# Streaming encoder on one core: order of the value products, of the first chunk's transfers and of the tail's convolution taps

## What is computed

```python
u = rmsnorm(x, g) @ w_in                     # 11 groups of 256 columns
a_b, a_c, a_x, a_g, b_v, b_a, b_g, c_u, c_g, x_q, x_g = split(u, 11)
y_a = a_b * conv3(a_c * a_x) * silu(a_g)
y_b = silu(layernorm(conv31(b_v * sigmoid(b_a)) + bias)) * silu(b_g)
y_c = (pool_linear(trailing_means(c_u) - c_u) + bias) * scale * silu(c_g)
y_x = softmax(q @ K.T / 8) @ V * silu(x_g)   # 4 heads, 256 memory tokens
y   = rmsnorm(x + concat(y_a, y_b, y_c, y_x) @ w_out, g_final)
```

## Time and profile before

| | |
|---|---|
| median of 3 runs | 1570.24 us (1567.27 to 1572.03) |
| the profiled execution | 1572.66 us |
| its span, first to last instruction | 1570.8 us |
| TensorE busy | 1447.3 us, 92% |
| VectorE busy | 1221.1 us, 78% |
| ScalarE, GpSimd busy | 566.9 us (36%), 234.0 us (15%) |
| TensorE's mean granted clock | 0.975 of full |

### The profile page before, as it was taken

One profiled execution on the slowest core, in us unless ns is written; L12 is line 12 of the kernel. 1 busy time (PEld: TensorE's weight loads), 2 busy tenths in 40 slices (PEclk: granted clock), 3 DMA queues, 4 the chain that ended last, 5 costly groups with the idle time before them and its releaser, 6 DMA issues.

```text
span 1570.8 us, 32694 instructions
## 1 busy us (share of the span) xinstructions
PE 1447.3 (92%) x11758; PEld 1238.1 (79%) x11758; DVE 1221.1 (78%) x3102; ACT 566.9 (36%) x1250; POOL 234.0 (15%) x188
## 2 busy tenths in 40 slices
PE   5877699999999999999999999999999999999995
PEld 4755587878787887878787887878787887878784
DVE  7996396886969696886969597886869697796856
ACT  7763232333324332342323332332333332333333
POOL 2251011111101111111001111111001111111110
PEclk9988799999999999999999999999999999999998
DMA  9875355555354556545354556445354556446373
GB/s 271 227 282 191 122 175 197 187 178 196 107 223 139 182 188 202 183 155 224 105 217 145 174 187 214 174 155 231 106 195 159 181 187 214 170 140 229 98 251 128
DMA packets 129827, 286.26 MB, mean 182 GB/s; under 512 B 12554, under 2 KB 70590, under 8 KB 129790
## 3 DMA queue, kind: packets, MB, share of 16 engines
q1 hardware_dynamic: 129789, 285.77, 53.6%
HBM read 226.65 MB, written 59.08 MB: 182 GB/s over the span
## 4 chain that ended last, share of the span: by engine, by line
PE 45%; DVE 26%; issue 14%; DMA 8%; ACT 2%; SPq 1%; POOL 1%; DVEq 1%; ACTq 0%; POOLq 0%
DVE z L1363 9%; PE u L524 7%; PE u L525 7%; PE u L526 7%; DMA pt<-probs_turned 4%; PE qps L524 4%; PE qps L526 4%; PE qps L525 4%; PE sps L524 4%; PE sps L526 4%; PE sps L525 4%; DVE prow L1387 3%; DMA probs_turned<-probs 3%; DVE xb L1291 2%; DVE probs L292 1%
## 5 line engine op out<-in xcount | busy, mean ns | idle before, releaser
L524 PE MATMUL u<-h_hi,w_hl 128*128 128x256 f16 (+1 forms) x2992 | 795.7, 272 | 12.1 <-ACT gate L872 7.3
L525 PE MATMUL u<-h_lo,w_hl 128*128 128x256 f16 (+1 forms) x2992 | 794.4, 271 | 0.0
L526 PE MATMUL u<-h_hi,w_hl 128*128 128x256 f16 (+1 forms) x2992 | 793.9, 271 | 0.0
L1363 DVE SCALAR_TENSOR_TENSOR z<-glu,cst,z 128x256 f32<-128x256 f32 (+1 forms) x1020 | 425.1, 488 | 0.5
L524 PEld LDWEIGHTS u<-h_hi,w_hl 128*128 128x128 f16 x2992 | 295.4, 99 | 63.7 <-issue 12.6
L526 PEld LDWEIGHTS u<-h_hi,w_hl 128*128 128x128 f16 x2992 | 295.6, 99 | 34.7
L525 PEld LDWEIGHTS u<-h_lo,w_hl 128*128 128x128 f16 x2992 | 295.6, 99 | 33.3
L872 ACT ACTIVATE gate<-u,inv 128x256 f32<-128x256 f32 (+1 forms) x204 | 83.0, 458 | 169.6 <-PE u L526 169.0
L524 PE MATMUL sps<-ring,y_hi 128*128 128x512 f32 (+1 forms) x278 | 112.4, 404 | 16.8 <-POOL y_lo L1805 14.3
L526 PE MATMUL sps<-ring,y_lo 128*128 128x512 f32 (+1 forms) x278 | 110.2, 396 | 0.0
L525 PE MATMUL sps<-ring,y_hi 128*128 128x512 f32 (+1 forms) x278 | 109.8, 395 | 0.0
(11 more groups left out here) (222 smaller groups left out, 1911.6 us busy)
## 6 DMA issues: line engine op xcount, KB each, us to landing
ring<-wo_split SPq DMA_DIRECT2D x256, 512.0 KB, 6.8
ob<-in_x_prompt SPq DMA_DIRECT2D x34, 512.0 KB, 4.3
probs_turned<-probs SPq DMA_DIRECT2D x130, 128.0 KB, 2.4
pt<-probs_turned SPq DMA_DIRECT2D x32, 512.0 KB, 3.4
out<-ob SPq DMA_DIRECT2D x32, 512.0 KB, 3.5
rows_turned<-rows SPq DMA_DIRECT2D x122, 128.0 KB, 2.4
w_hl<-in_w_in SPq DMA_DIRECT2D x20, 512.0 KB, 7.3
wo_split<-ring SPq DMA_DIRECT2D x16, 512.0 KB, 5.1
```

The source lines that it names most:

```text
L524: nc.tensor.matmul(out, a_hi, b_hi, start=first, stop=False)
L525: nc.tensor.matmul(out, a_hi, b_lo, start=False, stop=False)
L526: return nc.tensor.matmul(out, a_lo, b_hi, start=False, stop=last)
L1363: ins = nc.vector.scalar_tensor_tensor(z[:, c, 0:n], glu[:, c, k:k + n], w, z[:, c, 0:n], ALU.mult, ALU.add)
```

## The change

It moves steps and waits; nothing is computed otherwise, and no buffer is added.

- TensorE, chunks 1 to 15: a_g goes ahead of pair 0's value product; pair 1's goes from ahead of c_g to behind x_g and `z_rows`, right ahead of the out projection. In the sample chunk both go behind x_g and `z_rows`.
- Pair 1's `exps` waits for pair 0's transfers out instead of its transfer back. SyncE no longer waits for pair 1's transfer back before it loads the next rows into `xp`.
- Chunk 0: the last four `keep`s go between pair 0's transfers out and back; the last two ring loads go between the transfers of the two row tiles.
- ScalarE: `y_high` of y_b goes ahead of `row_hi` of tile 1, in chunk 0 ahead of both. VectorE, chunk 0: `yb_out` goes ahead of tile 1's rows.
- VectorE, sample chunk: the taps are spread otherwise.

```diff
             for p in range(RAW, PIECES):
                 keep(p - RAW)
                 load_piece(p)
-            for p in range(PIECES - RAW, PIECES):
-                keep(p)
...
+            def probs_leave(i, p, n):
+                sp.wait_ge(p_t_ok.sem, p_t_ok.at(i, p + 1))
+                put_out(probs_turned[p], turned_p, min(n, P), probs_out[p])
+
+            def probs_arrive(i, p, n):
                 m = min(n, P)
-                sp.wait_ge(p_t_ok.sem, p_t_ok.at(i, p + 1))
-                put_out(probs_turned[p], turned_p, m, probs_out[p])
                 sp.wait_ge(probs_out[p].sem, probs_out[p].at(i, 16 * (m // SQ)))
                 take_back(pt_w[p], probs_turned[p], m, pt_in[p])
...
             def first_sync(x_here, y_here, x_next, x_after):
-                for p in range(PAIRS):
-                    probs_across(0, p, N)
-                sp.wait_ge(pt_in[1].sem, 16)
+                probs_leave(0, 0, N)
+                for p in range(PIECES - RAW, PIECES):
+                    keep(p)
+                probs_arrive(0, 0, N)
+                probs_across(0, 1, N)
                 sp.dma_start(xp, x_next).then_inc(x_in[1].sem, 16)
                 sp.wait_ge(wlo_ok.sem, FT)
                 residual(0, N, x_here)
-                for q in range(RING, PIECES):
+                for q in range(RING, PIECES - 2):
                     ring_load(0, q)
-                for t in range(2):
-                    row_across(0, t, P)
+                row_across(0, 0, P)
+                for q in range(PIECES - 2, PIECES):
+                    ring_load(0, q)
+                row_across(0, 1, P)
...
                 for p in range(PAIRS):
                     probs_across(i, p, N)
-                sp.wait_ge(pt_in[1].sem, pt_in[1].at(i, 16))
                 sp.dma_start(xp, x_next).then_inc(x_in[1].sem, 16)
...
                 project(i, n, "a_b")
+                project(i, n, "a_g")
                 attend(i, n, 0)
-                project(i, n, "a_g")
                 mix(i, n)
                 project(i, n, "b_g")
-                attend(i, n, 1)
                 project(i, n, "c_g")
                 project(i, n, "x_g")
                 z_rows(i, n)
+                attend(i, n, 1)
...
                 project(CHUNKS, SAMPLE, "c_g")
+                project(CHUNKS, SAMPLE, "x_g")
+                z_rows(CHUNKS, SAMPLE)
                 for p in range(PAIRS):
                     attend(CHUNKS, SAMPLE, p)
-                project(CHUNKS, SAMPLE, "x_g")
-                z_rows(CHUNKS, SAMPLE)
...
                     if s >= 2:
-                        act.wait_ge(pt_in[0].sem, pt_in[0].at(i, 16))
+                        act.wait_ge(probs_out[0].sem, probs_out[0].at(i, 64))
...
                 z_silu(0, N)
+                y_high(0, N, 2, z[:, :, 0:N], yb_ok)
                 row_hi(0, *nxt[0])
                 row_hi(0, *nxt[1])
-                y_high(0, N, 2, z[:, :, 0:N], yb_ok)
...
                 row_turn(0, *nxt[0])
+                yb_out(0, N)
                 rows_rms(*nxt[1])
                 rows_scale(*nxt[1], rows=xp)
                 row_turn(0, *nxt[1])
-                yb_out(0, N)
...
-                taps(i, n, 0, 10)
+                taps(i, n, 0, 16)
                 q_low(i, n)
+                taps(i, n, 16, 21)
                 add_half(LAST, N, 0)
+                taps(i, n, 21, 24)
                 add_half(LAST, N, 1)
+                taps(i, n, 24, 26)
                 softmax_max(i, n, 0)
-                taps(i, n, 10, 14)
                 pool_diff(i, n)
+                taps(i, n, 26, 29)
...
-                taps(i, n, 14, 18)
+                taps(i, n, 29, TB)
                 ya_out(i, n)
-                taps(i, n, 18, TB)
```

More of the change, by code:

```diff
@@ L406, in row_across, with probs_across @@
                 take_back((xb, xp)[t], rows_turned[t], m, rows_in[t])
-            def probs_across(i, p, n):
+            def probs_leave(i, p, n):
+                sp.wait_ge(p_t_ok.sem, p_t_ok.at(i, p + 1))
+                put_out(probs_turned[p], turned_p, min(n, P), probs_out[p])
+            def probs_arrive(i, p, n):
                 m = min(n, P)
-                sp.wait_ge(p_t_ok.sem, p_t_ok.at(i, p + 1))
-                put_out(probs_turned[p], turned_p, m, probs_out[p])
                 sp.wait_ge(probs_out[p].sem, probs_out[p].at(i, 16 * (m // SQ)))
                 take_back(pt_w[p], probs_turned[p], m, pt_in[p])
+            def probs_across(i, p, n):
+                probs_leave(i, p, n)
+                probs_arrive(i, p, n)
             def residual(i, n, x_here):
@@ L472, in last_chunks @@
                     probs_across(LAST, p, N)
-                sp.wait_ge(pt_in[1].sem, pt_in[1].at(LAST, 16))
                 for src, off in ((cache_mem_k, 0), (cache_mem_v, GW)):
@@ L1209, in chunk @@
                 z_silu(i, N)
+                y_high(i, N, 2, z[:, :, 0:N], yb_ok)
                 row_hi(i, *nxt[1])
-                y_high(i, N, 2, z[:, :, 0:N], yb_ok)
                 out_squares(i, N, nxt[1][0])
```

## The result

The changed kernel took 1579.25 us (median of 6 runs, 1578.32 to 1582.34), the kernel before 1570.10 in 6 runs of its own: ratio 1.0063, 95% interval 1.0048 to 1.0078. It is slower by 9.2 us, 0.6%. The forecast was balance; the profiled execution took 1582.3 us, its span 1580.5, its mean granted clock 0.971.

The account below looks back on a forecast made before the run. TensorE, busy 92% of the span, was taken as the bound, its stalls and the slow clock behind them as the loss. Loop +20, chunk 0 -19, chunk 15 +2, sample chunk -3 sum to 0: 1570.5 us, range 1558 to 1583.

Parts of the forecast that it names:

- Old stalls go: Loop, TensorE: its waits for the probabilities ahead of both pairs' value products, 52.7 us in 32 waits, disappear.
- New stall before the fifth piece by the chain product, row turns, y_x: Loop: pair 1's later product delays VectorE's row turns 5.5 us, then y_x; TensorE waits 4.2 us per chunk (3.75 to 4.7).
- The 0.45 of holding by GpSimd: Loop, VectorE: a small operation of rows_rms is held 0.45 us by GpSimd's low half of y_c, on a shared port.
- Clock loss 1.4 per chunk (0.7 to 1.8): Loop: half-speed clock behind the new stall costs 1.4 us per chunk, with 0.7 and 1.8 as ends.
- Stall-free chunk 84.73: Loop: a chunk without its two stalls takes 88.30 - 0.95 - 2.62 = 84.73 us.
- Ring loads at nothing, 7 us of cover: Loop, SyncE: first ring load of the second eight leaves at 967.7, not 964.8; needed near 975, so it costs nothing.
- The loop: 14 loop chunks: 84.73 + 4.2 + 1.4 = 90.33 us against 88.89, +20 us in all (+4 to +33).
- Chunk 0, -19 (-15 to -21): Chunk 0: earlier transfers and y_high save 21 us, less 1.7 for the clock; -15 if transfers stay slow, -21 without clock loss.
- Chunk 15 +2, sample -3: Chunk 15: stalls go but a later gate and row path cost +2 us; sample chunk: earlier out projection gains 3 us.
- Sum 0: Whole kernel: +20 - 19 + 2 - 3 = 0, no change; within 0.3% given 42%.
- slower, dearer rows: Rival, 20%: stall of 4.7 always followed by a clock fall, or chunk 0's second row tile late as before; 1576 to 1583 us.
- slower, late ring loads: Rival, 12%: the ninth piece's weights land too late, costing TensorE 1 to 1.5 us per chunk; 1585 to 1591 us.

Follow-up runs that it names:

- e2: The changed kernel with the turned rows in other memory, free at that time, so that no row turn waits for a value product: 1503.74 us (0.9582).
- e7: The kernel before with only TensorE's new order of chunks 1 to 15; queue order, waits, chunk 0 and tail as before: 1596.13 us (1.0161).
- e5: The changed kernel with pair 1's value product of chunks 1 to 15 moved up between c_g and x_g: 1497.99 us (0.9537).
- e4: The changed kernel with 28 more matmuls, result never read, ahead of the fifth piece in chunks 1 to 15: 1577.02 us (1.0045).
- e3: The changed kernel with z_stats and yx_out ahead of the row turns on VectorE in the loop: 1594.15 us (1.0148).
- e8: The changed kernel with TensorE's order of chunks 1 to 15 as before; chunk 0, tail and waits as changed: 1553.97 us (0.9890).
- e6: e4 with four of SyncE's ring loads of the loop ahead of row tile 1's transfers: 1595.59 us (1.0147).

## Why the prediction was off by 9 us, point by point

The mechanism was right and its sizes were too kind; on a sum of large terms of opposite sign this moved the outcome from balance to slower. 1579.25 lies inside the stated 1558 to 1583, but the forecast was that nothing would change, at 1570.5, and that did not come.

- *Old stalls go*: right, all 52.7 us.
- *New stall before the fifth piece by the chain product, row turns, y_x*: right; e2 and e7 show it. VectorE stands 5.78 (5.5 said). TensorE's stall is 3.47 idle, 3.63 with the slower restart, instead of 4.2. The 0.45 of holding by GpSimd did not come in chunk 9: the operations that met GpSimd's of 958.94 to 960.23 were those of one input (L1272 took 0.11). In e5, where a one-column operation of two inputs met it, L1287 took 1.19. The Trainium skill, SBUF — State Buffer, on its two sides, lets only a VectorE operation with two SBUF inputs (or in a two-port mode) collide with GpSimd; these rows agree, and the prediction should have asked which operation of `rows_rms` would meet it. One input alone is no safe sign, though: in chunk 9 of the kernel before, L1269 of two columns took 1.22 at 963.70 beside GpSimd's 963.60, and takes 0.17 elsewhere; no row names its mode.
- *Clock loss 1.4 per chunk (0.7 to 1.8)*: too small. 51 us at half speed lose some 25 us, about 1.8 per chunk, the far end. But it is no loss that stands alone: the two chunks without a fall are as long, by waits for `ring`, and e4 got back 0.7 of it.
- *Stall-free chunk 84.73*: 85.11 (e2). Half of the 0.4 is the 0.17 that I added to each stall: one group takes 5.24, two with the step to the product 10.59 (e5), so a product without a wait begins some 5.35 behind its group's start. In rows 3's chunk it began 7.86 behind b_g's, so the stall of 2.45 cost about 2.5 and not 2.62, and pair 0's 0.84 and not 0.95. The rest no run assigns. The place of the product is not it, since e5, with another place, has 85.04 in its shortest chunks. Each of the 14 chunks pays it.
- *Ring loads at nothing, 7 us of cover*: wrong. The waits are small, 4.7 us in all, 5 of them in the loop with 0.48 to 0.78. But four of these five come in the two chunks whose clock did not fall, and e3, e4 and chunk 9 of e7 show the same: there was next to no cover left, not 7 us.
- The loop: 85.11 + 3.63 + 1.8 + 0.2 = 90.74, against 90.70 measured without chunk 1's 2.6. Predicted 90.33: +25.4 in place of **+20**. That it came so near is partly luck: the stall was 0.6 shorter, and stall-free length, clock and ring loads together 1.0 dearer.
- *Chunk 0, -19 (-15 to -21)*: -16.6 at b_a, less the 2.6 of half clock behind the stall, -14.0, just outside the range. The two moves worked as said: the exponentials' table load ran at 116.57, and no wait for y_b is left. The term that was mis-sized is tile 1's way out. Its turn ended at 151.3 instead of 149.2: the chain was 1 us less early than said, and here an operation was held by GpSimd for 0.9 (row below). Then queue and transfers out took from 151.3 to 159.8, 8.5 us, 7.6 of it the transfers, where 3.75 was taken from the loop, whose queue has no ring loads just ahead, with 1 to 2 for the full queue. From the turn's end to `row_hi` (163.49, row below) it is 12.2 us, nearly the 12.9 of before, the case that the end of -15 was for. What follows the transfers out took 1 less than said, and the half clock cost 2.6 instead of 1.7.
- *Chunk 15 +2, sample -3*: 0 to +1.3 and -3.0 (e7, e8); together -1.7, predicted -1.
- *Sum 0*: +25.4 - 14.0 - 1.7 = +9.7. Two terms failed by 5 us each: the loop's by clock, stall-free length and ring loads, chunk 0's by tile 1's way out and the clock behind its stall. The time lies in the case "slower, dearer rows" (20%), which came true by half: tile 1's way was nearly as slow as before and a fall followed in 12 of 14 chunks, but the stall was shorter than forecast, not 4.7. Part of "slower, late ring loads" (12%) was at work beside it.

Timelines of the changed kernel, chunk 0: VectorE, the held operation, and ScalarE, `row_hi` of tile 1. GpSimd's low half of y_b ran from 146.71 for 1.30; the operation's like takes 0.22.

```profile
146.89 1.14 DVE L1285 SCALAR_TENSOR_TENSOR st<-st 128x1 f32<-128x1 f32 x1
```

```profile
163.49 1.33 ACT L911 ACTIVATE h_hi<-probs 128x256 f16<-128x256 f32 x4 [7.71 <-DMA probs<-rows_turned]
```

Of the signs that the prediction named, the stalls before the fifth piece, VectorE's wait and the lower mean clock (0.971) were there. So was one that it had put under "wrong", waits for `ring`; and the first half of chunk 0 was added at 166.2, not near 163.

## What to carry to other kernels

Before a step is moved later, list what waits for its completion, through shared memory too, and where those waiters stand in their engine's order; then look for the slot between "its input has landed" and "its first waiter is ready". Here this slot was the end of c_g, and with the product in it the same change gave 4.6% instead of costing 0.6%. Ask then what was hidden behind the wait or the slow clock that you take away: here it was the ring loads. Ordering the waiters around the late step (e3) or loads around the transfers (e6) only handed the wait on.

## What the runs showed of the hardware

- The same small transfer out (four parts, 0.5 MB in all) takes 3.7 us with nothing in the queue ahead (kernel before, chunk 9), 5.5 and 7.6 in chunk 0 of the changed kernel behind six and two more ring loads, and 8.7 behind four of them (e6).
- How long a stall was did not decide whether the half clock followed. In the kernel before, pair 1's stalls of 1.98 to 2.31 were followed by it in six chunks, and those of 2.12 to 2.53 in the other eight were not. In the changed kernel it followed a stall of 3.46 in 12 of 14 chunks.
- With 28 unread matmuls in the stall no fall followed in the loop (e4), but more than half of the time that this should have given was lost again, in part in waits for loads.
- VectorE's one-column operations of two inputs take 0.16 to 0.22 us, and 1.12 to 1.19 where they met a GpSimd operation (L1281 in rows 7, L1285 above, L1287 in e5).
